# Attention kernel with three head groups: dividing the probability rows by their sums on VectorE ahead of the transposes, in place of turned inverse sums at the end of each group

## The chip, the cores and the metric

The kernel runs on one core of a Trainium2 chip. The metric is the device time of one execution in microseconds (us); lower is better. The engines are called as in the profile: PE is TensorE (PEld its weight loads), DVE is VectorE, ACT is ScalarE, POOL is GpSimd, SP is the engine that issues the DMAs.

## What is computed

One decoder layer on 1024 tokens of width 1024 in float32. After an RMS norm, one projection gives queries, keys, values and gates for sixteen heads of width 64 in three groups: A (eight heads, three dilated windows mixed by their softmax denominators), B (four heads that share keys and values, over the 256 best keys of an indexer) and M (four heads over 256 memory tokens). For every head the result is a softmax over scores, times values; then it is gated and projected:

```python
s = einsum('bthc,bmhc->bhtm', q, k) * Dh ** -0.5     # group M; A and B add a distance penalty and a mask
p = softmax(s, axis=-1)                              # exp(s - max) / sum
o = einsum('bhtm,bmhc->bthc', p, v)
...
o = concat([oA, oB, oM]) * silu(gate)
x = rms_norm(x + o @ w_out, g_final)
```

The division by the sum may stand before the product with the values (probabilities) or behind it (outputs); both give the same `o`.

## The kernel before, in words

**Pairs and steps.** The heads go in eight pairs, in the order M0, A0, A1, A2, A3, B0, B1, M1. A pair has eight query tiles of 128 tokens, so there are 64 steps, `s` from 0 to 63 (`STEPS`), eight to a pair. The two heads of a pair are called `a` = 0 and 1. In A and B step `i` of a pair looks at `i + 1` key tiles (128 to 1024 columns), in M always at two (256 columns). More than four key tiles are turned in two pieces (chunks).

**One step.** PE makes the scores of step `s` (`product`, line 1489). DVE adds the penalty or mask, writes the row to `prob` in SBUF and takes its extreme value (`add_bias`, 1266; 1253 for M). ACT takes the exponent in place, with the row sum into `lsum` (`exponent`, 988). One step later PE transposes `prob` into PSUM (`turn_prob`, 1560), ACT copies head 0 and DVE head 1 to `probT` (976 and 1275), and PE multiplies by the values into `o_ps` (`values`, 1586), a bank that holds four query tiles.

**Groups of four steps.** When four steps are through, DVE inverts their eight sums and spreads each over 64 columns into `linv` (`invert_sums`, 1284 and 1285). PE transposes `linv` into the bank `pt_ps[0]`, which `turn_prob` uses as well (`turn_sums`, 1608). DVE multiplies the gates by that bank (`finish_group`, 1293) and then by `o_ps` (1297). `turn_prob` of the next group and `turn_values` wait for 1293 (`linv_used`), because it reads the bank that they write.

**What sets the order.** Each engine runs its own fixed list, and semaphores join them. In step `s` PE does: scores of `s`; first chunk of `turn_prob` of `s - 1`; 24 matmuls of a projection (`fill`, 1434, the weights of later pairs; two halves around the second chunk where there are two); values of `s - 1`; now and then `turn_values`, `turn_sums`. DVE does: `add_bias` of `s`, `copy_probT` of `s - 1`, a first part of the top-k search, the second chunk's copy, `finish_group`, the low part of a projection (`split_low`, 1124), a second part of the search. The search (`choose`, lines 1189 to 1221) is a chain of DVE instructions that wait for each other; a table (`choice_plan`) puts one or two portions in each of two places of the steps 1 to 33. ACT makes the high part of the weights (`split_hi`, 814), POOL the low part (`split_lo`, 711) and the masks (762, 765). In the last eight steps the projections of the fill are those of the output (`project_out`, 1636 and 1642).

Of the kernel before, what the change touches and what calls it, by code (L numbers as in the profile page):

```python
# [15 lines left out]
P = 128  # L16
# [91 lines left out]
def pair_of_step(s):  # L108
    return s // NT, s % NT
# [197 lines left out]
def build_program(nc, x, mem, g_in, g_mem, w_in, w_mem, w_out, g_final, dist_tab, a_tab, out):  # L307
    with ExitStack() as ctx:
# [34 lines left out]
        linv = sb("linv", [P, 4, 2, DH])  # L343
# [101 lines left out]
        linv_ready = sem("linv_ready")  # L445
        linv_turned = sem("linv_turned")
        linv_used = sem("linv_used")
# [595 lines left out]
        def _(dve):  # L1043
# [233 lines left out]
            groups = [0]  # L1277

            def invert_sums(p, g):

                for a in range(2):
                    dve.wait_ge(prob_ready[a], p * NT + 4 * g + 4)
                inverse = lsum[:, p % 2, 4 * g:4 * g + 4, :]
                link(dve.reciprocal(inverse, inverse))
                dve.tensor_copy(linv[:, :, :, :], inverse.unsqueeze(3).broadcast_to([P, 4, 2, DH])).then_inc(linv_ready, 1)
                groups[0] += 1

            def finish_group(p, g):

                dve.wait_ge(gate_ready, sum(w <= W_OF["gate", p] for (what, _), w in W_OF.items() if what == "gate"))  # L1290
                dve.wait_ge(linv_turned, groups[0])
                cut = slice(HALF * g, HALF * g + HALF)
                dve.tensor_tensor(gates(p)[:, cut], pt_ps[0][:, :, :].rearrange("p a b -> p (a b)"),  # L1293
                                  gates(p)[:, cut], ALU.mult).then_inc(linv_used, 1)
                dve.wait_ge(linv_used, groups[0])
                dve.wait_ge(pv_done, CHUNK0[p * NT + 4 * g + 4])
                dve.tensor_tensor(gates(p)[:, cut], o_ps[:, :], gates(p)[:, cut], ALU.mult).then_inc(og_ready, 1)
# [25 lines left out]
            for s in range(STEPS + 1):  # L1323
# [11 lines left out]
                if s >= 1 and (s - 1) % 4 == 3:  # L1335
                    invert_sums(pair_of_step(s - 1)[0], (s - 1) % NT // 4)
# [3 lines left out]
                if s >= 1 and len(chunks(s - 1)) == 2:  # L1340
                    copy_probT(s - 1, 1)
                if early[1]:
                    add_out(*early[1])
# [28 lines left out]
        def _(pe):  # L1372
# [176 lines left out]
            def turn_prob(s, c):  # L1549
                g = CHUNK0[s] + c  # L1550
                for a in range(2):
                    pe.wait_ge(prob_ready[a], s + 1)
                    if g >= 1:
                        pe.wait_ge(pt_ready[a], g)
                    if a == 0 and s // 4 >= 1:
                        pe.wait_ge(linv_used, s // 4)
                    if a == 0 and c == 0 and v_turn_of_step(s):
                        pe.wait_ge(v_kept, v_turns_before(*v_turn_of_step(s)) + 1)
                    for n, k in enumerate(chunks(s)[c]):
                        last = pe.transpose(pt_ps[a][:, n, :], prob[:, a, s % 2, P * k:P * k + P], ident[:, :])  # L1560
                    last.then_inc(pt_done[a], 1)
# [28 lines left out]
            def turn_values(s):  # L1590
# [4 lines left out]
                if s // 4 >= 1:  # L1595
                    pe.wait_ge(linv_used, s // 4)
# [4 lines left out]

            def turn_sums(s):

                p, i = pair_of_step(s)
                pe.wait_ge(linv_ready, s // 4 + 1)
                pe.wait_ge(pt_ready[0], CHUNK0[s + 1])
                for c in range(4):
                    last = pe.transpose(pt_ps[0][:, c, :], linv[:, c, :, :].rearrange("p a f -> p (a f)"), ident[:, :])  # L1608
                last.then_inc(linv_turned, 1)
# [49 lines left out]
            for s in range(STEPS + 1):  # L1659
# [30 lines left out]
                if s >= 1 and (s - 1) % 4 == 3:  # L1690
                    turn_sums(s - 1)
# [47 lines left out]
```

## Time and profile before

| | us |
|---|---|
| median of 3 runs | 721.14 (720.52 to 722.98) |
| the profiled execution, its own time | 722.97 |
| its span | 721.2 |
| PE busy | 677.6 (94%) |
| DVE busy | 421.5 (58%) |
| ACT busy | 333.4 (46%) |
| POOL busy | 146.7 (20%) |

The span is the stretch between the first and the last instruction that the profile shows; the execution's own time is 1.8 us more. An engine's busy time is the sum of its instructions; since each engine runs in order, what matters is which engine the others wait for in each stretch of the span.

### The profile page before, as it was taken

What the parts mean: (1) busy time and instruction counts of PE and PEld (TensorE: products, weight loads), DVE (VectorE), ACT (ScalarE), POOL (GpSimd) and SP (SyncE); (2) the same over time, 40 slices, a digit from 0 to 9 for tenths busy, and PEclk for the clock granted to TensorE, in tenths of its full rate; (3) what the DMA queues carried; (4) which work ended last, traced back from release to release, by engine and by line L of the source; (5) the groups of instructions that cost most, each with busy time, mean ns of one, the idle gap of its engine ahead of it and who ended that gap; (6) DMA issues with size and microseconds to landing.
All of it is one profiled execution on the core that took longest, in us unless ns stands there. A gap on an engine that the chain in (4) does not pass through costs nothing.

```text
span 721.2 us, 11587 instructions
## 1 busy us (share of the span) xinstructions
PE 677.6 (94%) x4287; PEld 541.1 (75%) x4287; DVE 421.5 (58%) x985; ACT 333.4 (46%) x629; POOL 146.7 (20%) x96
## 2 busy tenths in 40 slices
PE   5999999999999999999998999999999999999992
PEld 4778887777778777777776787877888777777771
DVE  3947874396788477976698664542343354122245
ACT  5777653344335442534253434643563585121224
POOL 2021110111224013221124113210111166212102
PEclk9999999999999999999999999999999999999996
DMA  8511121111211121112111121101111416400004
GB/s 287 155 49 54 30 60 28 30 29 45 88 45 45 30 89 45 30 45 88 45 31 45 54 75 34 45 2 45 45 30 34 158 52 236 161 27 23 0 37 197
DMA packets 51863, 47.71 MB, mean 66 GB/s; under 512 B 5712, under 2 KB 44640, under 8 KB 51808
## 3 DMA queue, kind: packets, MB, share of 16 engines
q1 hardware_dynamic: 51808, 46.97, 21.2%
q8 instruction: 35, 0.57, 0.3%
q14 instruction: 20, 0.16, 0.1%
HBM read 39.62 MB, written 7.34 MB: 65 GB/s over the span
## 4 chain that ended last, share of the span: by engine, by line
PE 46%; DVE 12%; issue 3%; ACT 1%; DVEq 0%; ACTq 0%
PE j_ps L1434 13%; PE o_ps L1586 6%; PE pt_ps L1560 6%; PE s_ps L1636 5%; PE s_ps L1434 5%; PE s_ps L1489 4%; PE j_ps L1636 4%; DVE unread L1193 4%; DVE probT L1275 1%; PE s_ps L1642 1%; PE j_ps L1642 1%; DVE tk L1195 1%; DVE prob L1266 1%; PE pt_ps L1608 1%; DVE tk L1194 1%
## 5 line engine op out<-in xcount | busy, mean ns | idle before, releaser
L1434 PE MATMUL j_ps<-h_hi,w_hl 128*128 128x512 f32 (+2 forms) x656 | 213.4, 391 | 3.1 <-DVE h_lo L1068 1.2
L1434 PEld LDWEIGHTS j_ps<-h_hi,w_hl 128*128 128x128 f32 (+1 forms) x656 | 121.1, 186 | 28.7 <-issue 3.1
L711 POOL TENSOR_TENSOR w_hl<-w_raw,w_hl 128x1024 fp32r<-128x1024 f32 (+1 forms) x29 | 69.2, 2387 | 333.0 <-ACT w_hl L814 313.5
L988 ACT ACTIVATE prob<-prob,nmax 128x256 f32<-128x256 f32 (+7 forms) x128 | 90.0, 704 | 83.0 <-DVE nmax L1266 68.7
L1434 PE MATMUL j_ps<-h_lo,w_hl 128*128 128x512 f32 (+2 forms) x328 | 125.3, 382 | 0.0
L976 ACT ACTIVATE probT<-pt_ps 128x512 f32<-128x512 f32 (+3 forms) x88 | 41.3, 469 | 121.2 <-PE pt_ps L1560 120.6
L1560 PE MATMUL pt_ps<-ident,prob 128*128 128x128 f32 x496 | 73.8, 281 | 9.3 <-DVE gate L1293 5.0
L1560 PEld LDWEIGHTS pt_ps<-ident,prob 128*128 128x128 f32 x496 | 54.8, 141 | 27.0 <-issue 20.1
L1434 PE MATMUL s_ps<-h_hi,w_hl 128*128 128x512 f32 x224 | 74.1, 399 | 0.9 <-ACT qk L850 0.9
L1434 PEld LDWEIGHTS j_ps<-h_lo,w_hl 128*128 128x128 f32 (+1 forms) x328 | 61.1, 186 | 11.1
L1193 DVE TENSOR_SCALAR_CACHE_REDUCE unread<-idx,tk 128x384 uint8<-128x384 f32 (+5 forms) x72 | 67.8, 942 | 1.3
L1266 DVE CUSTOM_DVE_ANT_0 prob<-s_ps,bias 128x128 f32<-128x128 f32 (+7 forms) x64 | 47.0, 753 | 24.0 <-PE s_ps L1489 20.2
L1275 DVE COPY probT<-pt_ps 128x512 f32<-128x512 f32 (+3 forms) x88 | 46.6, 530 | 14.9 <-PE pt_ps L1560 14.4
L1124 DVE SCALAR_TENSOR_TENSOR qk<-j_ps,qk 128x512 fp32r<-128x512 f32 (+2 forms) x29 | 18.4, 635 | 53.8 <-ACT qk L850 38.9
L1434 PEld LDWEIGHTS s_ps<-h_hi,w_hl 128*128 128x128 f32 x224 | 42.5, 190 | 9.5 <-ACT qk L850 1.1
L1173 DVE SCALAR_TENSOR_TENSOR idx<-prob,w_i,idx 128x384 f32<-128x384 f32 (+5 forms) x42 | 41.9, 1039 | 10.2 <-ACT prob L926 10.1
L1434 PE MATMUL s_ps<-h_lo,w_hl 128*128 128x512 f32 x112 | 43.9, 392 | 0.0
L1586 PE MATMUL o_ps<-probT,v_sb 128*64 128x128 f32 x576 | 38.6, 278 | 3.3 <-DVE probT L1275 3.2
L1586 PEld LDWEIGHTS o_ps<-probT,v_sb 128*64 128x64 f32 x576 | 30.9, 136 | 14.0 <-issue 13.8
L1266 DVE CUSTOM_DVE_ANT_0 prob<-s_ps,idx 128x384 f32<-128x384 f32 (+5 forms) x24 | 21.0, 886 | 31.9 <-PE s_ps L1489 31.9
L1489 PE MATMUL s_ps<-qk 64*128 64x512 f32 (+3 forms) x288 | 34.8, 363 | 0.0
L1636 PE MATMUL s_ps<-h_hi,w_hl 128*128 128x512 f32 x96 | 31.9, 400 | 0.0
(242 smaller groups left out, 1071.2 us busy)
## 6 DMA issues: line engine op xcount, KB each, us to landing
w_raw<-in_w_in_dram SPq DMA_DIRECT2D x27, 512.0 KB, 4.1
idx<-in_x_dram SPq DMA_DIRECT2D x8, 512.0 KB, 6.2
bias<-in_a_tab_dram SPq DMA_DIRECT2D x8, 512.0 KB, 4.5
mixed_scratch<-gate SPq DMA_DIRECT2D x12, 256.0 KB, 2.5
bias<-in_x_dram SPq DMA_DIRECT2D x4, 512.0 KB, 6.5
probT<-in_w_mem_kv_dram SPq DMA_DIRECT2D x4, 512.0 KB, 6.3
bias<-in_w_out_dram SPq DMA_DIRECT2D x4, 512.0 KB, 3.7
out_dram<-idx SPq DMA_DIRECT2D x4, 512.0 KB, 4.2
```

The costliest lines, as they stand in the source:

```text
L711: pool.tensor_tensor(w_hl[:, w % 2, 1, :, 0:n], raw_of(w)[:, :, 0:n], w_hl[:, w % 2, 0, :, 0:n].bitcast(F32), ALU.subtract).then_inc(w_lo_ ...
L976: act.activation(probT[:, g % 2, 0, 0:n, :], pt_ps[0][:, 0:n, :], ACT.Copy).then_inc(pt_ready[0], 1)
L988: act.activation(prob[:, a, s % 2, 0:n], prob[:, a, s % 2, 0:n], ACT.Exp, scale=-1.0, bias=nmax[:, a, s % 2:s % 2 + 1], accum_out=lsum[:, ...
L1173: dve.scalar_tensor_tensor(out=x_slice(i), in0=relu[u % 4][:, 0:n], scalar=wt, in1=x_slice(i), op0=ALU.mult, op1=ALU.add).then_inc(idx_add ...
L1193: link(dve.tensor_scalar(unread[:, 0:n], xs, level, None, ALU.is_ge, ALU.add, accum_out=count))
L1266: dve.tensor_tensor_reduce(dst, s_ps[a][:, 0:n], table, scale, 3e38, ALU.add, ALU.min, low_out).then_inc(biased[a], 1)
L1275: dve.tensor_copy(probT[:, g % 2, 1, 0:n, :], pt_ps[1][:, 0:n, :]).then_inc(pt_ready[1], 1)
L1434: last = pe.matmul(bank[0:n, at:], a[:, k, 0:n], c[:, k, HALF * b + at:HALF * b + HALF], start=(k == 0 and q == 0), stop=(k == KD - 1 and ...
L1489: last[a] = pe.matmul(banks[a][:, keys], q[rows, tile], k[rows, keys], start=(m == 0), stop=(m == 2))
L1560: last = pe.transpose(pt_ps[a][:, n, :], prob[:, a, s % 2, P * k:P * k + P], ident[:, :])
L1586: last = pe.matmul(o_ps[DH * a:DH * a + DH, at], v, probT[:, g % 2, a, n, :], start=(k == 0), stop=(k == nk - 1))
L1636: pe.matmul(bank, a[:, p, :], wo_half(c, p, b), start=(p == 0 and q == 0), stop=False)
```

## The change

The sums are no longer turned. For every step and head DVE inverts the sum (one column) and multiplies the row of probabilities in SBUF by it, in place (`even_out`). `turn_prob` waits for that (`prob_even`) in place of the exponent (`prob_ready`). `invert_sums`, `turn_sums`, the multiplication by `pt_ps[0]` in `finish_group` and the three semaphores around them go, and with them the waits for `linv_used`.

```diff
+            def even_out(s, a):
+                p, i = pair_of_step(s)
+                total = lsum[:, p % 2, i, a:a + 1]
+                row = prob[:, a, s % 2, 0:P * key_tiles(s)]
+                dve.wait_ge(prob_ready[a], s + 1)
+                link(dve.reciprocal(total, total))
+                dve.tensor_scalar(row, row, total, None, ALU.mult).then_inc(prob_even[a], 1)
...
             def finish_group(p, g):
                 dve.wait_ge(gate_ready, sum(w <= W_OF["gate", p] for (what, _), w in W_OF.items() if what == "gate"))
-                dve.wait_ge(linv_turned, groups[0])
                 cut = slice(HALF * g, HALF * g + HALF)
-                dve.tensor_tensor(gates(p)[:, cut], pt_ps[0][:, :, :].rearrange("p a b -> p (a b)"),
-                                  gates(p)[:, cut], ALU.mult).then_inc(linv_used, 1)
-                dve.wait_ge(linv_used, groups[0])
                 dve.wait_ge(pv_done, CHUNK0[p * NT + 4 * g + 4])
...
-                if s >= 1 and (s - 1) % 4 == 3:
-                    invert_sums(pair_of_step(s - 1)[0], (s - 1) % NT // 4)
                 choose_portions(s, 0)
                 if early[0]:
                     add_out(*early[0])
                 if s >= 1 and len(chunks(s - 1)) == 2:
                     copy_probT(s - 1, 1)
+                if s < STEPS:
+                    even_out(s, 0)
+                    even_out(s, 1)
...
             def turn_prob(s, c):
                 g = CHUNK0[s] + c
                 for a in range(2):
-                    pe.wait_ge(prob_ready[a], s + 1)
+                    pe.wait_ge(prob_even[a], s + 1)
                     if g >= 1:
                         pe.wait_ge(pt_ready[a], g)
-                    if a == 0 and s // 4 >= 1:
-                        pe.wait_ge(linv_used, s // 4)
...
-                if s >= 1 and (s - 1) % 4 == 3:
-                    turn_sums(s - 1)
```

How the lists of the engines change is shown at two places. The first is DVE's list in step 20, the first step behind a group of pair A1, from the score rows of step 20 on (`prob,nmax<-s_ps,bias` is `add_bias`, `cut8` and `tk` belong to the search). Before:

```order
L1266 ISA prob,nmax<-s_ps0,bias 128x640 [waits pt_done_a,scored_a]
L1266 ISA nmax 128x1
L1275 COPY probT<-pt_ps 128x512 [waits pv_done,pt_done_b]
L1266 ISA prob,nmax<-s_ps1,bias 128x640 [waits pt_done_b,scored_b]
L1284 RECIPROCAL lsum<-lsum 128x8 [waits prob_ready_b,prob_ready_a]
L1285 COPY linv<-lsum 128x512 [waits dve_seq]
L1213 MAX cut8<-picked 128x8
L1214 SCALAR_TENSOR_TENSOR cut8<-eight,tk,cut8 128x8 [waits dve_seq]
L1216 TENSOR_SCALAR cut8<-eight,tk 128x8 [waits dve_seq]
L1217 SCALAR_TENSOR_TENSOR cut8<-cut8 128x8 [waits dve_seq]
L1293 TENSOR_TENSOR gate<-pt_ps,gate 128x512 [waits linv_turned,gate_ready,dve_seq]
L1297 TENSOR_TENSOR gate<-o_ps,gate 128x512 [waits pv_done,linv_used]
```

And with the change:

```order
L1263 ISA prob,nmax<-s_ps0,bias 128x640 [waits pt_done_a,scored_a]
L1263 ISA nmax 128x1
L1272 COPY probT<-pt_ps 128x512 [waits pv_done,pt_done_b]
L1263 ISA prob,nmax<-s_ps1,bias 128x640 [waits pt_done_b,scored_b]
L1210 MAX cut8<-picked 128x8
L1211 SCALAR_TENSOR_TENSOR cut8<-eight,tk,cut8 128x8 [waits dve_seq]
L1214 SCALAR_TENSOR_TENSOR cut8<-cut8 128x8 [waits dve_seq]
L1282 RECIPROCAL lsum<-lsum 128x1 [waits prob_ready_a,dve_seq]
L1283 TENSOR_SCALAR prob<-prob,lsum 128x640 [waits dve_seq]
L1282 RECIPROCAL lsum<-lsum 128x1 [waits prob_ready_b]
L1283 TENSOR_SCALAR prob<-prob,lsum 128x640 [waits dve_seq]
L1290 TENSOR_TENSOR gate<-o_ps,gate 128x512 [waits pv_done,gate_ready]
```

Three instructions of the group's end are gone. Four new ones stand behind the first part of the search and ahead of `finish_group`; such four stand at this place in each of the 64 steps.

The second place is PE's list, where `turn_prob` of a step begins. Before, from the values of step 19, the last of pair A1's first group, through the scores of step 21 to the turning of step 20:

```order
L1586 MATMUL o_ps<-probT,v_sb 64x128 [waits pt_ready_b,pt_ready_a]
L1586 MATMUL o_ps<-probT,v_sb 64x128 x7
L1608 MATMUL pt_ps<-ident,linv 128x128 [waits pt_ready_a,linv_ready]
L1608 MATMUL pt_ps<-ident,linv 128x128 x3
L1489 MATMUL s_ps0<-qk 128x512 [waits biased_b,biased_a]
...
L1560 MATMUL pt_ps<-ident,prob 128x128 [waits linv_used,pt_ready_a,prob_ready_a]
L1560 MATMUL pt_ps<-ident,prob 128x128 x3
```

With the change, at the scores and the turning of such a step:

```order
L1483 MATMUL s_ps0<-qk 128x512 [waits biased_b,biased_a]
...
L1552 MATMUL pt_ps<-ident,prob 128x128 [waits v_kept,pt_ready_a,prob_even_a]
L1552 MATMUL pt_ps<-ident,prob 128x128 x3
L1552 MATMUL pt_ps<-ident,prob 128x128 [waits pt_ready_b,prob_even_b]
```

The four transposes of `linv` are gone, the wait for `linv_used` too, and the wait for the exponent has become a wait for DVE's division.

## Rows read from the trace of the kernel before

**Rows 1.** The page: the chain that ended last, shares of the span by engine
```profile
PE 46%; DVE 12%; issue 3%; ACT 1%; DVEq 0%; ACTq 0%
```
**Rows 2.** Windows: length, busy PE, PEld, DVE, ACT, POOL, PE clock, DMA share, GB/s
```profile
273.19:307.98 34.79, 32.72 (x202) 25.50 (x202) 32.26 (x80) 15.10 (x29) 9.04 (x5) 1.00 0.14 39
348.92:386.26 37.34, 32.92 (x203) 25.60 (x203) 34.67 (x84) 14.97 (x29) 7.79 (x5) 1.00 0.13 36
```
**Rows 3.** Groups of instructions by shape: busy us, mean ns, idle before
```profile
L1293 DVE TENSOR_TENSOR gate<-pt_ps,gate 128x512 f32<-128x512 f32 x14 | 9.7, 692 | 36.6 <-PE pt_ps L1608 36.6
L1285 DVE COPY linv<-lsum 128x512 f32<-128x512 f32 x16 | 7.7, 480 | 0.5
```
**Rows 4.** Waits of PE: us in total, times, longest
```profile
PE o_ps L1586 <- DVE probT L1275: 6.9, 8, 1.8
PE pt_ps L1560 <- DVE gate L1293: 5.0, 9, 1.6
```
**Rows 5.** Timeline of PE: the end of pair A0, start us, length us
```profile
272.42 0.66 PE L1608 MATMUL pt_ps<-ident,linv 128*128 128x128 f32 x4
273.01 0.62 PE L1489 MATMUL s_ps<-qk 64*128 64x256 f32 x6
274.02 0.43 PE L1560 MATMUL pt_ps<-ident,prob 128*128 128x128 f32 x2 [0.40 <-DVE gate L1293]
```
**Rows 6.** One line's instructions: duration in ns, least, median, greatest
```profile
L1095 DVE TENSOR_SCALAR idx<-idx,stat x3: 748/748/754, 12.1 to 13.4; 128x1024 f32<-128x1024 f32 x3
L1194 DVE TENSOR_SCALAR tk<-tk,rungs x72: 211/214/216, 140.7 to 418.1; 128x1 f32<-128x1 f32 x72
L1058 DVE RECIPROCAL stat<-stat x5: 166/178/188, 11.2 to 710.9; 128x4 f32<-128x4 f32 x2, 128x2 f32<-128x2 f32 x1, 128x3 f32<-128x3 f32 x1, 128x5 f32<-128x5 f32 x1
```
**Rows 7.** Timeline of PE: turning of steps 7, 11, 18 and 20
```profile
191.59 0.66 PE L1560 MATMUL pt_ps<-ident,prob 128*128 128x128 f32 x4
...
222.74 0.66 PE L1560 MATMUL pt_ps<-ident,prob 128*128 128x128 f32 x4
...
288.73 0.87 PE L1560 MATMUL pt_ps<-ident,prob 128*128 128x128 f32 x6
...
307.98 0.74 PE L1560 MATMUL pt_ps<-ident,prob 128*128 128x128 f32 x5 [1.57 <-DVE gate L1293]
```
**Rows 8.** Timeline of DVE: last instructions before the new place, steps 7, 11, 18
```profile
192.67 0.28 DVE L1195 TENSOR_SCALAR tk<-tk,rungs 128x1 f32<-128x1 f32 x1
...
223.17 0.27 DVE L1195 TENSOR_SCALAR tk<-tk,rungs 128x1 f32<-128x1 f32 x1
...
289.93 0.27 DVE L1195 TENSOR_SCALAR tk<-tk,rungs 128x1 f32<-128x1 f32 x1
```
**Rows 9.** Timeline of DVE: step 16's group end, then step 20
```profile
273.19 0.69 DVE L1293 TENSOR_TENSOR gate<-pt_ps,gate 128x512 f32<-128x512 f32 x1 [4.54 <-PE pt_ps L1608]
...
304.74 2.37 DVE L1217 SCALAR_TENSOR_TENSOR cut<-cut 128x8 f32<-128x8 f32 x1
```
**Rows 10.** Timeline of POOL
```profile
288.66 2.41 POOL L711 TENSOR_TENSOR w_hl<-w_raw,w_hl 128x1024 fp32r<-128x1024 f32 x1 [6.94 <-ACT w_hl L814]
...
304.71 2.37 POOL L711 TENSOR_TENSOR w_hl<-w_raw,w_hl 128x1024 fp32r<-128x1024 f32 x1 [11.34 <-ACT w_hl L814]
...
382.40 3.25 POOL L762 TENSOR_SCALAR idx<-picked 128x896 f32<-128x896 f32 x1 [6.97 <-issue]
...
598.83 1.82 POOL L729 TENSOR_TENSOR w_hl<-picked,w_hl 128x768 fp32r<-128x768 f32 x1 [1.88 <-ACT w_hl L944]
```
**Rows 11.** Timeline of DVE beside the last two of those
```profile
383.13 0.50 DVE L1285 COPY linv<-lsum 128x512 f32<-128x512 f32 x1
...
599.73 1.21 DVE L1285 COPY linv<-lsum 128x512 f32<-128x512 f32 x1
```
**Rows 12.** Windows at the start of pair B0, columns as in rows 2
```profile
486.00:488.00 2.00, 0.54 (x6) 0.34 (x5) 1.84 (x7) 0.92 (x4) 0.10 (x1) 1.00 0.07 26
488.00:490.00 2.00, 2.00 (x12) 1.31 (x13) 0.22 (x1) 0.45 (x2) 0.00 (x0) 0.55 0.94 231
```

More of the change, by code:

```diff
@@ L342, in build_program @@
         lsum = sb("lsum", [P, 2, NT, 2])
-        linv = sb("linv", [P, 4, 2, DH])
         nmax = sb("nmax", [P, 2, 2])
@@ L444, in build_program @@
         pv_done = sem("pv_done")
-        linv_ready = sem("linv_ready")
-        linv_turned = sem("linv_turned")
-        linv_used = sem("linv_used")
+        prob_even = [sem("prob_even_a"), sem("prob_even_b")]
         og_ready = sem("og_ready")
@@ L1275, in copy_probT @@
                 dve.tensor_copy(probT[:, g % 2, 1, 0:n, :], pt_ps[1][:, 0:n, :]).then_inc(pt_ready[1], 1)
[L1277 to L1286, printed above, removed]
+            def even_out(s, a):
[5 more added lines that the diff above has]
+                dve.tensor_scalar(row, row, total, None, ALU.mult).then_inc(prob_even[a], 1)
             def finish_group(p, g):
                 dve.wait_ge(gate_ready, sum(w <= W_OF["gate", p] for (what, _), w in W_OF.items() if what == "gate"))
-                dve.wait_ge(linv_turned, groups[0])
                 cut = slice(HALF * g, HALF * g + HALF)
-                dve.tensor_tensor(gates(p)[:, cut], pt_ps[0][:, :, :].rearrange("p a b -> p (a b)"),
-                                  gates(p)[:, cut], ALU.mult).then_inc(linv_used, 1)
-                dve.wait_ge(linv_used, groups[0])
                 dve.wait_ge(pv_done, CHUNK0[p * NT + 4 * g + 4])
@@ L1594, in turn_values @@
                 pe.wait_ge(pt_ready[0], CHUNK0[s])
-                if s // 4 >= 1:
-                    pe.wait_ge(linv_used, s // 4)
                 n = P if PAIRS[p][0] == "A" else DH
@@ L1600, in turn_values @@
                 last.then_inc(v_turned, 1)
[L1602 to L1609, printed above, removed]
             def parts_of(p, t, b):
```

## The prediction
> **What bounds the kernel now.** I read the page first: PE is busy 94% of the span (the table above), and in the chain that ended last DVE is the only other engine with a share worth naming, 12% [rows 1]. So work taken from PE counts nearly in full, unless DVE, which gets all the new work, holds it up. Where that happens only the windows show. In the stretches 273.19 to 307.98 and 348.92 to 386.26 (steps 16 to 20 and 24 to 28, where the search has two portions in a place) DVE is busy 32.26 of 34.79 us and 34.67 of 37.34 us, and what is left are gaps between instructions that wait for each other [rows 2]. These stretches are bounded by PE and DVE at once. The search ends at step 33, and behind it PE alone sets the pace.
>
> **What goes.** On PE the four turnings of a group cost it 0.59 us (272.42 to the scores at 273.01) [rows 5]. The bank's release through `linv_used` made PE wait 5.0 us in nine places [rows 4], mostly 0.40 each as at 274.02 [rows 5], once 1.57 [rows 7]. On DVE each group loses a reciprocal (priced below), a copy (480 ns in the mean), together 0.6 us with their overlap, and the product with the bank (692 ns, 0.7 us) [rows 3]. DVE idled 36.6 us in front of that product [rows 3]; this idle time doesn't vanish, since 1297 then waits for the values in its place.
>
> **What comes.** 128 reciprocals of one column and 128 products in SBUF. The nearest reciprocals have 2 to 5 columns and take 166 to 188 ns; I take 0.17 and 0.04 us of gap. The product is the operation of line 1095, 748 ns for 1024 columns, and of line 1194, 214 ns for one [rows 6]: so 0.22 us and 0.52 ns for each column, of which 0.07 overlap with what follows. One head costs 0.21 + 0.15 + 0.52n/1000 us, a step with both heads 0.99 us at 256 columns, 1.12 at 384, 1.25 at 512, 1.39 at 640. All 64 steps hold 63,488 columns: 128 x 0.36 + 33 = 79 us more on DVE, less 16 x 1.30 = 21. The bound above is the product with two inputs, 692 ns for 512 columns [rows 3], 0.92 ns a column; that would be 25 us more. Line 1095 is the same operation on the same memory, so I take its value.
>
> **Where it lands.** Sums over the whole span say nothing here; the question is, step by step, whether `even_out` is through when PE wants to turn. The place is known: DVE's last instruction ahead of it has a time in the trace, and so has the start of the turning. Head 1 may come later by the turning of head 0 (0.11 us per tile). I did this for all 64 steps, with pairs of rows like those of rows 7 and 8.
> - Steps 0 to 6 and 12 to 16, 21 to 24, 29 to 32, 34 to 63: it is through 0.1 to 6 us before it is wanted. Nothing is lost but where noted below.
> - Step 7: DVE reaches the place at 192.95 [rows 8], done 193.94; PE is at head 1 at 191.81 [rows 7]: 2.1 us late.
> - Steps 10 and 11: at step 11 DVE comes at 223.44 [rows 8], done 224.69, wanted 223.18 [rows 7]: 1.5 late, and step 10's own division (1.12) stands ahead of it: 2.6.
> - Step 18: DVE at 290.20 [rows 8], done 291.32, wanted 289.06 [rows 7]: 2.3 late, and so all the way from 17 to 20: PE follows DVE. So what counts is how much longer DVE's list gets between the group end at 273.19 and step 20. It starts 0.6 + 0.7 = 1.3 earlier; steps 17 to 19 add 0.99 + 1.12 + 1.25 = 3.4; the 0.6 goes. In step 20 the place is reached at 307.11 [rows 9], done 308.50, wanted 308.42 [rows 7]: 0.1. Together 0.1 - 1.3 + 3.4 - 0.6 = 1.6 us later than now.
> - Steps 25 to 28 are built alike (0.1 late at step 28): 1.6.
> - Step 33: 1.1 late, less the 1.3 of the group end: -0.2.
> The first stretch is 2.1 (step 7) + 2.6 (step 11) less two group ends at 1.0 (0.59 and a wait of 0.40) and one at 0.6: 2.1. Up to step 33 the sum is 2.1 + 1.6 + 1.6 - 0.2 = **+5.1 us**, savings counted.
>
> After step 33 PE is alone: seven group ends at 0.59 and two waits of 0.40 are 4.9 us. In the tail the copy, the reciprocal and the product of the last group go from the path to the end: 1.3. **-6.2 us.** Without anything else the change is worth -1.1 us.
>
> **POOL.** A third thing is not in these sums. In step 20 an instruction of 8 columns on DVE took 2.37 us; it began at 304.74 [rows 9], just behind a POOL tensor_tensor of 304.71, and ended with it [rows 10]. A small instruction takes some 0.2 [rows 6]. A copy of 512 columns from SBUF to SBUF, 0.48 in the mean of sixteen [rows 3], took 1.21 beside a POOL tensor_tensor from 598.83 to 600.65 [rows 10, 11]. The new product is of the copy's kind, one SBUF source at two columns for the price of one. POOL's tensor_tensor (2.4 us) starts when ACT's `split_hi` is through, about 1 us behind the exponent; where DVE lags, `even_out` comes 2 to 3 us behind the exponent, into it. Step 18: POOL from 288.66 to 291.07 [rows 10], DVE at 290.4: 0.7 us held. I count seven such meetings in steps where PE has nothing to spare (2, 6, 8, 10, 18, 26, 28) and one more in the late stretch (54). From above one costs the whole 2.4 us, from below nothing; I take 0.8, less than half an operation, as part is spare: **+6.5 us**.
>
> The Trainium skill (SBUF — State Buffer, section "SBUF: two separate sides") says that VectorE in a two-port mode or with two SBUF inputs and GpSimd share a pair of ports as an exclusive lock for the whole instruction. The trace agrees for tensor_tensor on POOL, with the 2.37 and the 1.21 us above. By that rule POOL's one-input mask instructions (line 762) would hold the product too, and the sum would be some 2 us more; the trace has a copy of line 1285 that took 0.50 in the middle of one of 3.25 us [rows 10, 11], so my sum leaves them out.
>
> **Sum.** +5.1 - 6.2 + 6.5 = +5.4 us on the profiled execution's 722.97, that is 728.4. That execution is 1.8 above the median of 721.14; on the median it is **726.5 us**.
>
> **Rivals.**
> - *No meetings with POOL* (0.20). The order shifts, the divisions slip past, or PE has room for them: -1.1, 720.0 us. For it: rows show only two holds in all, at 304.74 and at 599.73. Against: the lagging steps put the division just where POOL works.
> - *PE's savings come through* (0.13). The lag feeds on itself less than I think: PE also loses 6.9 us waiting for DVE's copy at the values [rows 4], and a PE that is held at the turning no longer waits there; and the 2.2 us of hold at 304.74 may go, as that instruction moves 0.6 us ahead, out of POOL's reach. With both, the early part falls from +5.1 to about 0, meetings cost 2: -4 to -8, 715 us. It decides if DVE reaches the place of steps 17 to 20 less than 1.5 us later than PE. Against: DVE has no idle time in those stretches [rows 2], so work added there comes out at the end.
> - *PE's clock* (0.12). Behind a stretch with PE busy 0.54 of 2 us the granted clock was 0.55 for the next 2 us, which is for the most part the lower of its two levels [rows 12]. Holds of 2 us in each of steps 17 to 19 and 25 to 27 may bring that about: 1 to 2 us each in four or five places, 733 us. Against: the longest wait of that kind, 1.8 us [rows 4] in the second of the two stretches, left its clock at 1.00 [rows 2].
> - *The product runs at the two-input rate* (0.05): 0.4 ns more for 3,584 columns in each of three stretches is 4.3 us, longer holds come to it: +6, 733 us.
> The list of instructions shows that the change does what it says, so that is no rival.
>
> **How the numbers follow.** The forecast has 0.50, its own range 722 to 732. Two tenths may lie outside: 717 takes in all but the better half of the second rival, 737 the third and fourth with some meetings more. About 0.3% (2.2 us) is what a measurement of this kernel can tell from no change. Faster: 0.13 and a little of the first rival, 0.15. Same: the rest of the first rival and the low end of the forecast, 0.22. Slower: 0.63.
>
> **What would show it.** PE without L1608 and without waits for the gate product. New waits of `turn_prob` for DVE's product, 2 us each at steps 7, 10, 11, 17 to 20, 25 to 28 and hardly any from 34 on; some 12 to 18 us in all, against 8 us less idle and 9 less work elsewhere. DVE busy about 480 us. Products at 0.35 us for 256 columns, 0.75 for 1024, and a few of 1.5 to 3 us beside POOL. The time from step 34 to the end 6 us shorter. It is wrong if PE's waits for the division come to under 8 us, or if the late part doesn't shrink.

## The result, and the profile after the change

The changed kernel takes **733.82 us** (median of 4 runs, 733.49 to 734.99); beside it the kernel before took 721.47 (4 runs, 720.52 to 722.98). The ratio is 1.016 (95% interval 1.014 to 1.018): 12 us more than before, where the prediction said 5. The profiled execution's span is 732.2 us, 11.0 more than before's 721.2.

The page of the changed kernel: busy time of the engines, the chain that ended last, and three of the costliest groups (busy us, mean ns of one | idle before it).

```profile
PE 677.2 (92%) x4223; PEld 537.5 (73%) x4223; DVE 504.8 (69%) x1193; ACT 333.5 (46%) x629; POOL 147.6 (20%) x96
...
PE 45%; DVE 14%; issue 3%; ACT 1%; DVEq 0%; ACTq 0%
...
L708 POOL TENSOR_TENSOR w_hl<-w_raw,w_hl 128x1024 fp32r<-128x1024 f32 (+1 forms) x29 | 69.6, 2402 | 340.4 <-ACT w_hl L811 328.1
...
L1552 PE MATMUL pt_ps<-ident,prob 128*128 128x128 f32 x496 | 78.5, 286 | 24.2 <-DVE prob L1283 19.9
L1283 DVE TENSOR_SCALAR prob<-prob,lsum 128x256 f32<-128x256 f32 (+7 forms) x128 | 95.4, 745 | 4.5
```

DVE is busy 504.8 us (before: 421.5), and its share of the chain rose from 12% [rows 1] to 14%. PE has 64 matmuls fewer and is still busy as long as before. (In step 20 the search's line 1213, 0.23 us, still runs between 1211 and 1214, though DVE's list with the change leaves it out.) The products (line 1283) took 745 ns in the mean, and the turning (line 1552) stood 24.2 us idle, most of it waiting for them.

The waits of PE that answer to [rows 4] (us in total, times, longest), and the reciprocals by themselves (least, median, greatest ns):

```profile
PE pt_ps L1552 <- DVE prob L1283: 19.9, 16, 3.0
PE o_ps L1578 <- DVE probT L1272: 3.4, 4, 1.2
PE pt_ps L1552 <- DVE probT L1272: 2.1, 5, 1.0
```
```profile
L1282 DVE RECIPROCAL lsum<-lsum x128: 143/156/165, 134.2 to 700.6; 128x1 f32<-128x1 f32 x128
```

The 5.0 us for the gate product are gone, the wait for the copies fell from 6.9 to 3.4, and a new wait of 19.9 us took their place.

**Where the time came from** shows when both traces are laid side by side. A row gives the place on PE just ahead of the turning of that step, which is where the scores of the next step start, minus the same place in the kernel before (worked out from PE's timelines; us). Where the text says that a step starts earlier or later, it means this place. The columns of the experiments are used further down.

| step | before | changed | no division | one column | POOL behind | ACT divides | ACT in 13 steps |
|---|---|---|---|---|---|---|---|
| 7 | 191.10 | +1.6 | -1.3 | -1.3 | +0.3 | -0.5 | -1.6 |
| 16 | 273.01 | +6.8 | -3.2 | +1.7 | +2.8 | +0.9 | -2.1 |
| 24 | 348.74 | +8.4 | -6.5 | +0.8 | +3.0 | +0.9 | -4.5 |
| 29 | 395.15 | +16.5 | -8.6 | +0.7 | +8.6 | +1.7 | -3.8 |
| 34 | 442.55 | +16.5 | -9.6 | +0.4 | +8.5 | +3.5 | -3.8 |
| 44 | 514.51 | +14.0 | -13.6 | -3.6 | +4.5 | +9.9 | -7.8 |
| 60 | 655.34 | +11.6 | -16.4 | -6.4 | +2.1 | +14.3 | -10.1 |
| span | 721.2 | +11.0 | -17.0 | -7.0 | +1.5 | +13.7 | -10.8 |

The changed kernel loses 8.4 us up to step 24, another 8.1 in steps 24 to 28 alone, and wins 5.5 from step 34 to the end. Steps 24 to 28 are where the prediction had 3.2. Three timelines show what happened in step 28 (start, length in us, and in brackets PE's wait). DVE:

```profile
396.68 1.53 DVE L1283 TENSOR_SCALAR prob<-prob,lsum 128x640 f32<-128x640 f32 x1
398.13 0.15 DVE L1282 RECIPROCAL lsum<-lsum 128x1 f32<-128x1 f32 x1
398.31 2.45 DVE L1283 TENSOR_SCALAR prob<-prob,lsum 128x640 f32<-128x640 f32 x1
```

POOL in the same microseconds:

```profile
392.41 3.26 POOL L759 TENSOR_SCALAR idx<-picked 128x896 f32<-128x896 f32 x1 [8.33 <-DVEq L1233]
395.76 2.10 POOL L762 TENSOR_TENSOR idx<-idx,dist 128x896 f32<-128x896 f32 x1
397.82 2.59 POOL L708 TENSOR_TENSOR w_hl<-w_raw,w_hl 128x1024 fp32r<-128x1024 f32 x1
```

And PE's turning of the two heads:

```profile
398.26 0.66 PE L1552 MATMUL pt_ps<-ident,prob 128*128 128x128 f32 x4 [1.38 <-DVE prob L1283]
400.82 1.11 PE L1552 MATMUL pt_ps<-ident,prob 128*128 128x128 f32 x4 [1.90 <-DVE prob L1283]
```

A product of 640 columns that nothing holds takes 0.55 us. These two are held: the first ended with the mask's second instruction (line 762), the second with `split_lo` (line 708). PE waited for each. Windows of 2 us behind it and behind a like hold in step 26 (length, busy PE, PEld, DVE, ACT, POOL, PE clock, DMA share, GB/s):

```profile
374.00:376.00 2.00, 0.23 (x2) 0.00 (x0) 1.90 (x5) 0.10 (x1) 2.00 (x1) 0.97 0.00 0
376.00:378.00 2.00, 0.76 (x4) 0.74 (x5) 1.97 (x4) 0.00 (x0) 0.96 (x1) 0.50 0.00 0
378.00:380.00 2.00, 2.00 (x8) 1.71 (x7) 1.86 (x6) 0.49 (x1) 0.00 (x0) 0.50 0.92 239
...
398.00:400.00 2.00, 0.66 (x4) 0.42 (x4) 1.97 (x3) 0.60 (x1) 2.00 (x1) 0.95 0.04 8
400.00:402.00 2.00, 1.18 (x5) 1.19 (x6) 2.00 (x3) 0.00 (x0) 0.41 (x1) 0.50 0.00 0
402.00:404.00 2.00, 2.00 (x6) 1.51 (x6) 1.89 (x5) 0.00 (x0) 0.00 (x0) 0.50 0.75 187
```

Behind 2 us with PE busy 0.23, and behind 2 us with PE busy 0.66, the granted clock went to 0.50, the lower of its two levels, and stayed there while PE had work again. There are three such places (3.4 us from 195 on, 6.8 us each from 376 and from 400 on); between its start and its last 11 us the kernel before has only that of [rows 12], 3.4 us long.

### The profile page after: what moved, and what is told of

It reads as the page before. It is cut to its first block, busy times and chain, and to the rows that moved or that the text cites. A ratio compares the mean times of both kernels' runs of the same rounds, so it can differ in the third digit from the quotient of the medians.

```text
span 732.2 us, 11620 instructions
## 1 busy us (share of the span) xinstructions
PE 677.2 (92%) x4223; PEld 537.5 (73%) x4223; DVE 504.8 (69%) x1193; ACT 333.5 (46%) x629; POOL 147.6 (20%) x96
## 4 chain that ended last, share of the span: by engine, by line
PE 45%; DVE 14%; issue 3%; ACT 1%; DVEq 0%; ACTq 0%
PE j_ps L1428 13%; PE o_ps L1578 6%; PE pt_ps L1552 5%; PE s_ps L1617 5%; PE j_ps L1617 5%; PE s_ps L1428 4%; PE s_ps L1483 4%; DVE unread L1190 3%; DVE prob L1283 3%; DVE prob L1263 1%; DVE probT L1272 1%; PE s_ps L1623 1%; PE j_ps L1623 1%; DVE tk L1192 1%; PE s_ps L1637 1%
## 5 line engine op out<-in xcount | busy, mean ns | idle before, releaser
L1428 PE MATMUL j_ps<-h_hi,w_hl 128*128 128x512 f32 (+2 forms) x656 | 216.7, 396 | 3.1 <-DVE h_lo L1065 1.2
L1428 PEld LDWEIGHTS j_ps<-h_hi,w_hl 128*128 128x128 f32 (+1 forms) x656 | 123.3, 189 | 29.5 <-issue 3.1
L1428 PE MATMUL j_ps<-h_lo,w_hl 128*128 128x512 f32 (+2 forms) x328 | 127.0, 387 | 0.0
L1552 PE MATMUL pt_ps<-ident,prob 128*128 128x128 f32 x496 | 78.5, 286 | 24.2 <-DVE prob L1283 19.9
L1283 DVE TENSOR_SCALAR prob<-prob,lsum 128x256 f32<-128x256 f32 (+7 forms) x128 | 95.4, 745 | 4.5
L1428 PE MATMUL s_ps<-h_hi,w_hl 128*128 128x512 f32 x224 | 74.6, 402 | 0.9 <-ACT qk L847 0.9
L1170 DVE SCALAR_TENSOR_TENSOR idx<-prob,w_i,idx 128x384 f32<-128x384 f32 (+5 forms) x42 | 41.9, 1039 | 10.2 <-ACT prob L923 10.1
L1263 DVE CUSTOM_DVE_ANT_0 prob<-s_ps,idx 128x384 f32<-128x384 f32 (+5 forms) x24 | 21.0, 886 | 20.8 <-PE s_ps L1483 20.4
```

The source lines that it names most:

```text
L1170: dve.scalar_tensor_tensor(out=x_slice(i), in0=relu[u % 4][:, 0:n], scalar=wt, in1=x_slice(i), op0=ALU.mult, op1=ALU.add).then_inc(idx_add ...
L1263: dve.tensor_tensor_reduce(dst, s_ps[a][:, 0:n], table, scale, 3e38, ALU.add, ALU.min, low_out).then_inc(biased[a], 1)
L1283: dve.tensor_scalar(row, row, total, None, ALU.mult).then_inc(prob_even[a], 1)
L1428: last = pe.matmul(bank[0:n, at:], a[:, k, 0:n], c[:, k, HALF * b + at:HALF * b + HALF], start=(k == 0 and q == 0), stop=(k == KD - 1 and ...
```

## Experiments

**1. No division at all.** `even_out` is left out and the turning waits for the exponent, so the outputs are not normalised. This is the floor: only what the change removes.

```diff
-                if s < STEPS:
-                    even_out(s, 0)
-                    even_out(s, 1)
...
-                    pe.wait_ge(prob_even[a], s + 1)
+                    pe.wait_ge(prob_ready[a], s + 1)
```

> The changed kernel without the division (the output is not divided by the sums): it measures what the removals alone are worth. If the late part's 6.2 us and the early group ends add up as I reckoned, 15.2 us below the kernel before, 706 us. If PE is held by DVE's search in steps 17 to 20 and 25 to 28 in any case, the early savings stay away and it comes to 710 to 714 us.

Measured: 706.37 us, ratio 0.978 (0.976 to 0.981), as reckoned. The removal is worth 15 to 17 us (15.1 against the 721.47 of the first comparison, 16.7 against the 723.09 beside this run), 7.4 of it from step 34 on. DVE's busy time is 20.8 us less than before's, as the prediction had it (21).

**2. Reciprocals, but products of one column.** The rows stay undivided but for their first column.

```diff
-                row = prob[:, a, s % 2, 0:P * key_tiles(s)]
+                row = prob[:, a, s % 2, 0:1]
```

> The changed kernel with the division of one column only (the other columns are left undivided): reciprocals, number of instructions, place and waits stay, the 33 us of columns go. Theory of DVE's length: steps 17 to 19 add 2.2 in place of 3.4 us, steps 7 and 11 are still 1.8 and 1.3 late, so some 3 us less from the chain itself, 730 us. If POOL's holds and PE's clock are behind most of the loss, a one-column product isn't held and 5 to 9 us more go: 722 to 726 us.

Measured: 715.27 us, 0.990 (0.987 to 0.993), 8.9 above the floor and below both expectations: the columns, with all that hangs on them, cost the changed kernel 18.5 us. PE's waits for the product:

```profile
PE pt_ps L1552 <- DVE prob L1283: 11.0, 10, 1.8
```

So more than half of the waits are there with 256 instructions that do next to nothing (27.4 us of products, 20.2 of reciprocals). None of these products took over 218 ns, though many lay beside POOL.

**3. POOL's `split_lo` behind the division.** The full computation; the meetings with `split_lo` are taken away.

```diff
                 while next_w < min(coming(s) + 2, N_W):
+                    pool.wait_ge(prob_even[1], s + 1)
                     split_lo(next_w)
```

> POOL's low part of the weights waits until the division of its step is through, so that the two can't meet; nothing else changes. Theory of the holds (about 21 us of held products, eight of them on PE's path): 733.8 less 6 to 9, 725 to 728 us. Theory of DVE's length alone: within 1 us of 733.8. If POOL's delay itself makes PE wait for weights, slower than 734.

Measured: 724.18 us, 1.002 (1.000 to 1.004): 9.6 less than the changed kernel. The products alone:

```profile
L1284 DVE TENSOR_SCALAR prob<-prob,lsum 128x256 f32<-128x256 f32 (+7 forms) x128 | 73.0, 570 | 4.5
```

They fell from 95.4 to 73.0 us, and no PE instruction waits for POOL's weights. Up to step 33 two held products are left, one of 0.7 us too much in step 0, which PE didn't wait for, and one in step 28, by the mask's two-input instruction, which the edit does not touch; the first row is POOL's, the second DVE's, the windows behind it show the clock at 0.54 and 0.60:

```profile
391.37 2.19 POOL L763 TENSOR_TENSOR idx<-idx,dist 128x896 f32<-128x896 f32 x1
```
```profile
391.74 2.17 DVE L1284 TENSOR_SCALAR prob<-prob,lsum 128x640 f32<-128x640 f32 x1
```
```profile
392.00:394.00 2.00, 0.38 (x5) 0.14 (x2) 2.00 (x2) 0.60 (x1) 1.57 (x2) 1.00 0.00 0
394.00:396.00 2.00, 2.00 (x7) 1.73 (x8) 1.93 (x5) 0.00 (x0) 2.00 (x1) 0.54 0.31 119
396.00:398.00 2.00, 2.00 (x7) 1.61 (x6) 1.97 (x5) 0.70 (x1) 0.36 (x1) 0.60 0.22 42
```

**4. PE kept busy.** Twelve transposes of the identity, whose result nobody reads, stand ahead of the turning in eight lagging steps, so that PE works while it would wait.

```diff
+LAGGING = [7, 10, 11, 17, 18, 25, 26, 28]
...
+                    if a == 0 and c == 0 and s in LAGGING:
...
+                        for n in range(12):
+                            pe.transpose(pt_ps[0][:, n % 4, :], ident[:, :], ident[:, :])
+                    pe.wait_ge(prob_even[a], s + 1)
```

> In the eight steps where PE waits for the division it first does 12 idle transposes (1.5 us) into the bank that it is about to fill. Theory of the clock: the granted clock stays at 1.00 in 190 to 200, 370 to 384 and 400 to 408 and the time falls by 4 to 7 us, 727 to 730 us. If the clock matters nothing, the transposes cost what they exceed the wait, 734 to 737 us.

Measured: 732.4 us, 1.014 (1.011 to 1.017), between the two expectations and not clear of the changed kernel's 733.82 (1.014 to 1.018). In the trace the clock is full in all of the early part, but a drop of 3.4 us that the changed kernel doesn't have comes at 501.6:

```profile
372.00:382.00 10.00, 8.43 (x53) 6.33 (x52) 9.58 (x23) 3.18 (x8) 3.27 (x1) 1.00 0.21 53
...
392.00:402.00 10.00, 7.59 (x61) 5.95 (x60) 9.26 (x15) 3.87 (x7) 7.92 (x3) 1.00 0.00 0
...
501.60:505.00 3.40, 3.23 (x16) 2.41 (x17) 2.28 (x10) 1.27 (x6) 0.00 (x0) 0.51 0.89 236
```

Step 33 starts 13.4 us behind the kernel before in place of 15.4. So the clock costs 2.0 us there, all of it in steps 26 to 28 (the drop at 195 cost 1.2 at step 8, and that was gone by step 10, where both stand within 0.1). Of these 2.0 the new drop takes 1.1 back, and 0.9 is left at the end of the span. The clock is part of the miss, not the whole.

**5 and 6. Is it the place of the new wait?** Both keep experiment 3's wait on POOL. In 5 POOL's masks wait too, and where a step has two portions of the search, the division stands ahead of the last one. In 6 PE does not wait for the division at all: the products are made, but written into the other step's buffer, so PE turns undivided rows. So that no row is overwritten too soon, two waits of DVE come in as well; in the trace DVE never stands at the product for them.

```diff
-                choose_portions(s, 0)
+                if split_here(s):
...
+                    for n, slot in mine[:-1]:
+                        choose(IDX_TILES[n], slot)
+                    even_out(s, 0)
+                    even_out(s, 1)
+                    for n, slot in mine[-1:]:
+                        choose(IDX_TILES[n], slot)
```

> With POOL's weights and masks behind the division (as in the run of POOL's wait, 724.2 us), the division stands behind the first portion of the search's place 0 in place of the last, where there are two: about 1.6 us sooner in steps 17 to 20 and 25 to 28. Theory of the place (PE waits because the division stands late in DVE's step): 4 to 8 us less, 716 to 720 us. Theory of DVE's length (its list in the stretch is too long wherever the division stands): 721 to 724 us.

```diff
-                dve.tensor_scalar(row, row, total, None, ALU.mult).then_inc(prob_even[a], 1)
+                dve.tensor_scalar(prob[:, a, (s + 1) % 2, 0:P * key_tiles(s)], row, total, None, ALU.mult).then_inc(prob_even[a], 1)
...
-                    pe.wait_ge(prob_even[a], s + 1)
+                    pe.wait_ge(prob_ready[a], s + 1)
```

> DVE does the same reciprocals and products, but writes them into the buffer of the other step, where nobody reads them, and PE turns the undivided rows as soon as the exponent is through (POOL waits as in 724.2 us). DVE's length is all there, the new wait of PE is gone. Theory of the length: 720 to 724 us. Theory of the new wait: PE no longer follows DVE step by step, only the group's end and the copies bind them, 710 to 715 us.

Measured: 721.44 us (0.999, 0.998 to 1.000) and 722.24 us (0.999, 0.997 to 1.000), against 724.18 for experiment 3. PE's waits in experiment 5, then in 6:

```profile
PE o_ps L1593 <- DVE probT L1278: 9.9, 10, 2.0
PE pt_ps L1567 <- DVE prob L1289: 6.3, 8, 2.7
```
```profile
PE o_ps L1583 <- DVE probT L1275: 13.9, 12, 2.2
PE pt_ps L1557 <- DVE probT L1275: 5.6, 6, 3.6
```

Both times are those of the theory of length. With the new wait gone altogether only 2 us come back. PE then waits for DVE's copies instead, 19.5 us. In these stretches PE follows the length of DVE's list, whichever instruction it waits for.

One hold is still in both, and the waits above don't separate it from the length: in step 28 the mask's second instruction, which the extra wait did not move out of the way, held the first product (experiment 5, POOL's row, then DVE's). It is the longest wait of 5, 2.7 us, and in 6 the like one (2.45 us) makes late the copy for which PE then waits 3.6. Behind each the clock is at 0.50 for 3.4 us.

```profile
390.55 2.07 POOL L768 TENSOR_TENSOR idx<-idx,dist 128x896 f32<-128x896 f32 x1
```
```profile
390.56 2.41 DVE L1289 TENSOR_SCALAR prob<-prob,lsum 128x640 f32<-128x640 f32 x1
```

**7 and 8. Less search where DVE is full.** The search's portions of three steps of the A pairs are spread, with the division (7, with POOL's waits) and in the kernel before (8).

```diff
-    return [(1, 1), (2, 2), (2, 2), (2, 2), (1, 1), (1, 1), (1, 1), (1, 1)][i]
+    return [(1, 1), (2, 1), (2, 1), (2, 1), (1, 1), (1, 1), (1, 1), (1, 1)][i]
```

> The changed kernel with POOL's wait and the second place of three steps of each A pair given one portion of the search in place of two, so that it ends at step 40 in place of 33. DVE's list from the group's end to step 20 and to step 28 gets some 5 us shorter, more than the 3.4 that the divisions add. Both theories of DVE: the waits in the early part all but go, 711 to 716 us. If something else holds PE there, 720 us or more.

> The kernel before with the same spread search, as a control: in the kernel before PE loses some 5 us to DVE in the two stretches (1.6 and 0.7 for the gates, 3 for the copies), so 717 to 720 us. If the spread itself is what speeds the run before up, as much as 10 us less.

Measured: 721.72 us (0.999, 0.997 to 1.001) and 727.33 us (1.007, 1.005 to 1.009). Neither came out as expected: 7 lies where something else should hold PE, and 8 is slower than the kernel before, not faster. The steps show where. In 7 step 29 starts 3.4 us earlier than in the kernel before (8.6 later in experiment 3), and step 44 starts 2.1 later. In 8 step 29 starts 6.3 us earlier, and step 44 starts 4.6 later: the search now ends near the start of pair B0, and PE stands there. The rows are those of 8, the last one a window:

```profile
484.76 1.98 PE L1586 MATMUL o_ps<-probT,v_sb 128*64 128x128 f32 x16 [3.51 <-DVE probT L1275]
491.62 0.69 PE L1586 MATMUL o_ps<-probT,v_b 128*64 128x128 f32 x4 [2.23 <-DVE probT L1275]
...
484.00:497.20 13.20, 10.20 (x49) 7.67 (x50) 5.64 (x15) 2.94 (x10) 0.40 (x1) 0.50 0.23 60
```

So DVE's work in steps 16 to 28 holds PE back in the kernel before as well, and this way of moving it later only moves the loss. The loss is more than the two waits: behind the first one the clock stays at its lower level for 13.7 us, where the kernel before has 3.4 there [rows 12]. How much of the 7.3 us lost from step 39 to 44 is the clock's was not tried apart; 10.3 us more at half speed would be 5 at most.

**9 and 10. ACT makes the products.** DVE keeps one reciprocal of both sums of a step (two columns); ACT multiplies, ahead of its other work of the step (9) or at the end of it (10). The whole result is computed.

```diff
+                act.wait_ge(inverted, s + 1)
+                for a in range(2):
+                    row = prob[:, a, s % 2, 0:P * key_tiles(s)]
+                    act.activation(row, row, ACT.Copy, scale=lsum[:, p % 2, i, a:a + 1]).then_inc(prob_even[a], 1)
```

> DVE makes one reciprocal of both sums of a step (128x2) behind the first portion of the search; ACT makes the two products in place, as copies with a scale, behind the high part of the weights and ahead of its copy of head 0; PE turns as before the product is through on ACT. The whole result is computed. Theory (what costs is that the products and 128 reciprocals lengthen DVE's list where it is saturated, that they meet POOL's two-input instructions, and nothing else): DVE's new work falls from some 96 + 20 us to some 11, no product is held by POOL, and the time is that of the kernel without any division (706.4) plus half or less of what the one-column kernel added (8.9): 708 to 713 us, faster than the kernel before. Rival (the new link exponent, sum, product before the turning is what costs, on whatever engine): ACT has 0.3 to 1.0 us of product per head, and a reciprocal from DVE to wait for, which comes later than its own exponent; PE then waits 10 to 20 us for ACT's products, the copies of head 0 come later too: 718 to 726 us.

> As the run before it, but ACT's two products stand at the end of its step, behind its copies of head 0 and what it evacuates, so that nothing of ACT's older work waits for DVE's reciprocal. Theory (length of DVE's list): again 708 to 713 us, within 3 us of the other place; whichever of the two places lets PE wait less is the faster one. Rival (latency of the new link): here the products come later still, PE waits for them in nearly every step where two chunks leave little room, 722 us or more, and the difference between the two places is over 5 us.

Measured: 737.39 us (1.020, 1.018 to 1.022) and 762.67 us (1.055, 1.053 to 1.057). The theory failed as I had put it. Of the rival the wait came true (14.7 us in 9, expected 10 to 20) and the distance between the two places, but 737.39 us is far above its 718 to 726. The engines' busy time and PE's wait in 9, and the wait in 10:

```profile
PE 678.3 (92%) x4223; PEld 537.3 (73%) x4223; DVE 408.5 (56%) x1001; ACT 409.8 (56%) x757; POOL 145.4 (20%) x96
...
PE pt_ps L1566 <- ACT prob L996: 14.7, 25, 1.5
```
```profile
PE pt_ps L1567 <- ACT prob L996: 38.0, 41, 2.3
```

DVE is at 408.5 us, less than before the change, and the kernel is slower still. But the table says where: up to step 28 experiment 9 stands within 2 us of the kernel before, and it loses 10 of its 13.7 us from step 34 on, where the kernels with the products on DVE win. The length of DVE's list is the price only where DVE is full. Elsewhere it is what ACT's products bring with them, and that is more than one thing: from 445 us on PE waits 3.8 us for the products themselves (the link exponent, reciprocal, product) and 5.3 for ACT's copies of head 0, which stand behind them in ACT's list, and the clock drops four times for 3.4 us. They were not tried apart.

**11 and 12. ACT only where DVE is full.** From that reading: ACT makes the products in steps 7 to 11, 17 to 20 and 25 to 28 (11), or in all up to 33 (12); DVE in the others, with POOL behind it. Both compute the whole result. POOL's wait stands only in the steps where DVE divides.

```diff
+ON_ACT = [*range(7, 12), *range(17, 21), *range(25, 29)]
...
+                    if s not in ON_ACT:
+                        pool.wait_ge(prob_even[1], s + 1)
...
+                    if s in ON_ACT:
+                        even_out(s)
```

> ACT makes the two products (and DVE one reciprocal of both sums) in steps 7 to 11, 17 to 20 and 25 to 28 alone, the steps that the prediction names as full on DVE; in all others DVE divides as in the changed kernel, and POOL's split_lo waits for it. The whole result is computed. The kernel with ACT everywhere stood 0.4 to 1.9 us behind the kernel before in steps 20 to 28 and lost its time from step 36 on, where ACT makes the search's and the weights' work and DVE has room; the kernel with POOL behind the division lost 7.5 us up to step 33 and gained 5.3 from there to step 60. Theory (each engine loses only where its own list is full): +1 to +3 us at step 33, -5.3 behind it and -1.3 in the tail: 716 to 720 us against 721.5 to 723, faster than the kernel before by 0.3 to 0.7%. Rival (DVE's list is full in the steps between too, so that what is taken from it in thirteen steps comes back in the next ones): +5 us or more at step 33, 721 to 724 us.

> As the run before it, with ACT's products in all steps 0 to 33 and DVE's from 34 on. Theory: up to step 33 the +3.0 us of the kernel with ACT everywhere, behind it the -5.3 and -1.3 of DVE's division: 718 to 721 us, within 2 us of the other version and not faster than it. Rival as there: if the steps between are what fills DVE, this one is faster than the other by 2 us or more.

Measured: **712.27 us** (4 runs), 0.985 (0.983 to 0.987) for 11, and 721.86 us, 0.998 (0.997 to 1.000) for 12. Version 11 beats both kernels: 10.7 us faster than the kernel before beside it (722.93) and, by the ratios, 3% faster than the changed one. PE's waits for the division:

```profile
PE pt_ps L1583 <- ACT prob L999: 4.3, 6, 1.1
...
PE pt_ps L1583 <- DVE prob L1303: 1.5, 4, 0.8
```

19.9 us of waiting have become 5.8, and no window of 5 us between 130 and 620 shows a clock under 0.97. The rival (DVE full in the steps between too) is refuted: 12 takes the division from DVE in those steps as well and is 9.6 us slower than 11, where I had expected 2 at most. For 11 I had expected 716 to 720: step 34 starts 3.8 us earlier than before in place of 1 to 3 later, since ACT's products in thirteen steps cost PE 4.3 us, where in all 34 (experiment 12) they cost 10.9.

## Why the prediction was right and wrong

The forecast was 726.5 us, with 722 to 732 as its own range; 733.82 lies above that, where the prediction had put the rivals of the clock and of the two-input rate. In the traces it is +11.0 us against +5.4.

- **The sign and the place: right.** PE waits for the new product, 19.9 us (predicted 12 to 18), in the early part, and the late part gets shorter.
- **Prices: right.** Products without their holds took 61.4 us (95.4 less 34.0, the time above 0.22 us + 0.52 ns a column); from the prediction's figures it is 61.2. So the product doesn't run at the two-input rate, and that rival is out. A reciprocal is 156 ns (predicted 170). DVE's 504.8 us less the 34.0 are 471 (predicted 480).
- **After step 33: right.** Predicted -6.2 us, measured -5.5. Each quiet group end gave 0.58 to 0.59, as [rows 5] said. From step 39 to 42 before's own clock drop [rows 12] does not recur, which the prediction didn't count (experiments 1 and 2 win 2.8 there, 2.2 more than the group end); the changed kernel wins only 1.3 there, with a product of 2.43 us at 499.64 and waits of 1.0 and 0.8 us around it.
- **Up to step 24: right in sum.** The steps of the prediction are +2.1, +1.6 and five meetings at 0.8, 7.7 us; measured 8.4. Experiment 3, without the meetings with `split_lo`, stands at +3.0, with 3.7 predicted, so the meetings cost 5.4 and not 4.0: a little luck is in the sum.
- **Steps 25 to 28: the failed step.** Predicted was +1.6 ("built alike") and two meetings (26 and 28) at 0.8, 3.2 us; measured 8.1. These 4.9 us are nearly the whole miss in the trace (11.0 measured, 5.4 forecast). PE waited 3.0 us in step 26, 1.38 and 1.90 in step 28. Three terms were mis-sized. The clock stood in no term of the sum; experiment 4 puts it at 2.0 (8.1 against 6.1 with PE kept busy). The list was more than 1.6: experiment 3, without the meetings with `split_lo`, still loses 5.6 here, of which 1.62 is the wait for the product that the mask held, and an estimated 1.7 the clock (two windows of 2 us at 0.54 and 0.60), which leaves some 2.3. The rest of the 8.1, some 3.8 us, is holds. "I take 0.8, less than half an operation, as part is spare" was too small where nothing was spare, and the mask's second instruction, a tensor_tensor like `split_lo`, was not counted at all: the held products were 1.45 us too long in step 26, 0.98 (by the mask) and 1.90 in step 28. This split of the 8.1 is an estimate from three traces; each experiment alone shows only its own difference.
- **The count of meetings: wrong.** There are 25 held products, 34.0 us too long in all (24 by a two-input instruction of POOL, one beside a one-input one), and fourteen of 20.6 us up to step 33, where I counted seven. The lag that the division makes is what carries it into POOL's time. By experiment 3 the meetings with `split_lo` cost 9.6 us, their part of the clock included; predicted was 6.5 for all (eight at 0.8 are 6.4).
- **The rival on PE's clock** came in beside the forecast, not in place of it: three drops, 2 us in all, not 1 to 2 in each of four or five places. I had argued against it from a wait of 1.8 us; waits of 3.0, and of 1.38 and 1.90 close together, did it, and at 195 one of 1.93 not far behind one of 0.36.
- **The rival "PE's savings come through"** got one thing right, the wait for the copies fell by 3.5 us, but the time did not come back.
- **What is left is DVE's list:** 8.9 us from reciprocals and 256 instructions (experiment 2), 8.9 more with the columns (experiment 3 above it), against 15 to 17 saved. The second figure isn't the columns' alone: 5.7 of it fall in steps 24 to 28, where experiment 3 has the mask's hold and a clock drop and experiment 2 has neither.

How the 2 us of clock divide between the meetings and the longer list was not tried apart. Experiment 2, in which no product is held, has the first of the three drops (at 193 us) and not the other two.

## What to carry to other kernels

Work moved from the engine that bounds a kernel to one with 58% busy is only free where that engine's windows have room: here the same work given to a third engine in thirteen steps of 64 alone took the kernel with POOL's wait from 724.2 to 712.3 us, 11 us faster than before the change, and given to it in all steps made it 14 us slower than before. Count every meeting of a fast VectorE copy or product with a two-input GpSimd instruction, the masks' too, and price it whole where the waiting engine has nothing to spare. Where such waits add up, put the clock's drop into the sum and not among the rivals.

## What the runs showed of the hardware

- **POOL's two-input instruction holds a product of 128 columns, but not one of one column.** Products of 128 to 1024 columns ended with POOL's instruction; a 128-column one took 2.43 us (first row DVE, then POOL, both of the changed kernel). The reciprocals of the changed kernel never took over 165 ns, the products of one column of experiment 2 never over 218.

```profile
440.10 2.43 DVE L1283 TENSOR_SCALAR prob<-prob,lsum 128x128 f32<-128x128 f32 x1
```
```profile
440.06 2.38 POOL L708 TENSOR_TENSOR w_hl<-w_raw,w_hl 128x1024 fp32r<-128x1024 f32 x1 [13.83 <-ACT w_hl L811]
```

- **The hold works the other way too.** POOL's instruction took 3.26 us in place of 2.4 when it began 0.02 us behind a DVE instruction with two SBUF sources (first row DVE, then POOL). The Trainium skill (SBUF — State Buffer, section "SBUF: two separate sides") gives the shared ports to whichever starts first, VectorE with two SBUF inputs or GpSimd, and these rows agree: POOL would have had to wait 1.07 us, and it took some 0.9 longer. It is the instruction that then held the product of step 26, so this hold was lengthened by DVE's own search.

```profile
373.68 1.09 DVE L1202 SCALAR_TENSOR_TENSOR picked<-picked,idx 128x896 f32<-128x896 f32 x1
```
```profile
373.70 3.26 POOL L708 TENSOR_TENSOR w_hl<-w_raw,w_hl 128x1024 fp32r<-128x1024 f32 x1 [11.80 <-ACT w_hl L811]
```

- **A one-input instruction of POOL slows a product that starts beside its beginning, but doesn't hold it to its end.** A product of 512 columns (0.49 by itself) took 1.07 us beside one of 3.70. By that same section the product would be blocked until POOL's end, 3.4 us later; these rows show 0.6 us. The prediction had left these instructions out, on a copy that took 0.50 [rows 11]; that was closer, though the cost isn't nothing.

```profile
463.61 1.07 DVE L1283 TENSOR_SCALAR prob<-prob,lsum 128x512 f32<-128x512 f32 x1
```
```profile
463.31 3.70 POOL L759 TENSOR_SCALAR idx<-picked 128x1024 f32<-128x1024 f32 x1
```

One row doesn't fit: in experiment 7 a product of 128 columns that began 2.4 us into such an instruction took 0.90 us in place of 0.29 and ended with it. What decides is not shown. First row DVE, then POOL:

```profile
423.14 0.90 DVE L1285 TENSOR_SCALAR prob<-prob,lsum 128x128 f32<-128x128 f32 x1
```
```profile
420.70 3.25 POOL L761 TENSOR_SCALAR idx<-picked 128x896 f32<-128x896 f32 x1 [7.42 <-issue]
```
